# Weighting and turning the prompt's attention outputs during the sample's scores, in a four-layer decoder step on one core

## The chip, the cores and the metric

The program runs on one core of a Trainium2 chip. The metric is the device time of one execution in microseconds (us), the median of several runs; lower is better.

## What is computed

One inference step of a four-layer trunk for two groups of tokens that share the weights: a prompt of 512 tokens and a sample of 8 sequences with 4 new tokens each, 544 columns in all. Layers 0 and 3 are attention layers, layer 1 is a gated delta rule, layer 2 a pooling; each is followed by an MLP. Only the attention layers matter here. Cut to that:

```python
for g, (window, dil) in enumerate(((128, 1), (512, 4), (2048, 16))):   # 3 groups of 6 heads of 64
    q, k, v = rope(qkv[g, 0]), rope(qkv[g, 1]), qkv[g, 2]
    o, lse = dilated_window_prompt(q, k, v, window, dil)     # prompt: no cache
    o, lse = dilated_window_sample(q, k, v, cache_g, window, dil)   # sample: cached keys and values
wts = softmax(stack(lses), over the 3 groups)                # per token and head
y = (stack(outs) * wts).reshape(B, T, 1152) @ w_out          # out-projection, 1152 -> 1024
```

## The kernel before

Activations lie transposed, channels on the 128 partitions and the 544 tokens along the row. Every large product is done in three float32r passes: each operand is split into a high part (a Copy on ScalarE, `act_hi` or `w_hi`) and the rest (a subtraction on VectorE, `act_lo` or `w_lo`), and `pe_tile` (L210) multiplies hi by hi, lo by hi and hi by lo. A weight tile has `t.kt` blocks of 128 rows (9 in the out-projection) and is done by two matmuls of 272 columns for each pass and block, six matmuls a block. `sp_weights` loads the raw weights on SyncE's queue, `act_split` (L188) and `dve_split` (L195) split them two tiles ahead.

The engines have queues of their own in an order written out by hand, and meet at semaphores. In an attention layer (`MixA`) that order is, for each engine:

1. In-projection: 27 weight tiles in 9 units (3 groups by 3 pairs of heads), with the prompt's attention of one unit worked in between the tiles of the next. The prompt's outputs lie unweighted in `a_o` (tokens on the partitions), the negative maxima and sums of their softmax in `a_st`. The new keys and values leave in `prompt_rows` and `sample_rows` on SyncE's queue.
2. The sample's scores: 12 units of cached keys (`K_UNITS`: units 0 and 1 of group 0, units 2 to 9 of group 1, units 10 and 11 of group 2). TensorE does `turn_keys(i + 1)` (L926: 12 transposes of 128x128 from the cache buffer `s_kv` to `misc[1]` to `misc[3]`), then `sample_scores(i)` (L939 and L944). ScalarE copies the three turned tiles of each unit to `s_kT` (L1085), and `turn_keys(i + 2)` waits until the three copies of unit i + 1 are done. VectorE masks the scores and takes the maxima once for each of six pairs of group and batch (L1218 to L1223), ScalarE takes the exponentials (L1071). GpSimd issues the loads of the next cached keys and values into five buffers.
3. The sample's weights: `combine(0, 2, ...)` (L1231 to L1244, one exponential of ScalarE in its middle at L1091) and the scaling of the sample's probabilities (L1252).
4. On TensorE the sample's probabilities are turned (L962, L966) and multiplied with the cached values (L974, L978, L985). Meanwhile VectorE combines the prompt's weights. Group 0 holds tokens in natural order on the partitions, groups 1 and 2 in order modulo 4, so the softmax numbers go through DRAM (`scratch0`, `scratch1`) and come back in the other order (`a_stx0`, `a_stx1`); SyncE issues that between the mask's load and the first out-projection weights. Then VectorE weights `a_o` in place (L1263).
5. The sample's outputs are turned (L993), and split to `act_hi` (L1109) and `act_lo` (L1268).
6. The prompt's outputs: nine tiles f, each turned by four transposes (L1001) to `misc[f % 2]`, split by ScalarE (L1112) and VectorE (L1272) straight from there. Tile f waits until VectorE is through with tile f - 2. `prompt_cols` writes tiles 0 to 2 as they lie and tiles 3 to 8 with a step of four elements (16 bytes).
7. TensorE waits for all nine `act_lo` tiles, then does the eight weight tiles of the out-projection (`a_out`), each evacuated by VectorE's addition to `x` (L1278). The norm and the MLP follow.

## Time and profile before

| | |
|---|---|
| median of 3 runs | 3223.58 us (3214.03 to 3229.64) |
| the profiled execution's own time | 3220.44 us |
| its span, first to last instruction | 3218.6 us |
| busy: TensorE, VectorE, ScalarE, GpSimd | 94%, 44%, 29%, 19% |
| mean granted TensorE clock | 0.926 of full |

The time outside the span is 1.84 us. In the rows "PE" is TensorE's matmul, "PEld" its weight load, DVE is VectorE, ACT ScalarE, POOL GpSimd, SPq SyncE's DMA queue. L followed by a number is a line of the kernel. A row of instructions in order of time reads: start us, us, engine, line, operation, out<-in, xcount, and in brackets the idle time before it and what ended it. PEclk is the share of the full clock that was granted, 0.50 and 1.00 being its two levels, 1.2 and 2.4 GHz. Attention stage 2 runs from 270.68 to 321.79 us in layer 0 and from 2643.43 to 2694.31 us in layer 3.

### The profile page before, as it was taken

What the parts mean: (1) busy time and instruction counts of PE and PEld (TensorE: products, weight loads), DVE (VectorE), ACT (ScalarE), POOL (GpSimd) and SP (SyncE); (2) the same over time, 40 slices, a digit from 0 to 9 for tenths busy, and PEclk for the clock granted to TensorE, in tenths of its full rate; (3) what the DMA queues carried; (4) which work ended last, traced back from release to release, by engine and by line L of the source; (5) the groups of instructions that cost most, each with busy time, mean ns of one, the idle gap of its engine ahead of it and who ended that gap; (6) DMA issues with size and microseconds to landing.
All of it is one profiled execution on the core that took longest, in us unless ns stands there. A gap on an engine that the chain in (4) does not pass through costs nothing.

```text
span 3218.6 us, 55286 instructions
## 1 busy us (share of the span) xinstructions
PE 3019.4 (94%) x24181; PEld 2832.1 (88%) x24181; DVE 1403.1 (44%) x1904; ACT 933.9 (29%) x1634; POOL 616.6 (19%) x518
## 2 busy tenths in 40 slices
PE   7998799999999899999999993999999988899998
PEld 6996599999999777768999993999999983899998
DVE  4552443334675322243433347443356542443332
ACT  5554222222334211112322221222225542322222
POOL 0001141123210111002321142322140002322213
PEclk9998799999999866668999995999999988999999
DMA  3236333343323000212333330443332246234332
GB/s 106 74 89 187 109 99 125 124 131 115 95 75 82 2 1 1 54 53 60 119 120 124 122 113 24 130 128 125 120 124 64 83 133 193 61 120 127 123 125 98
DMA packets 440935, 318.48 MB, mean 99 GB/s; under 512 B 17181, under 2 KB 427470, under 8 KB 438359
## 3 DMA queue, kind: packets, MB, share of 16 engines
q1 hardware_dynamic: 430967, 277.19, 28.4%
q0 software_dynamic: 9728, 37.75, 3.7%
q8 instruction: 191, 3.13, 0.4%
q14 instruction: 49, 0.40, 0.0%
HBM read 299.62 MB, written 71.68 MB: 115 GB/s over the span
## 4 chain that ended last, share of the span: by engine, by line
PE 86%; DVE 6%; ACT 3%; issue 2%; DMA 2%; SPq 1%; POOL 0%; ACTq 0%; DVEq 0%; POOLq 0%
PE acc L210 66%; PE acc L939 2%; PE misc L926 1%; PE misc L1677 1%; PE misc L1678 1%; PE misc L883 1%; PE acc L1665 1%; PE misc L1628 1%; PE acc L1664 1%; PE misc L1639 1%; PE misc L1526 1%; PE acc L1680 1%; DMA s_kv<-cache_a_kv 1%; ACT a_sw L1063 1%; PE misc L829 1%
## 5 line engine op out<-in xcount | busy, mean ns | idle before, releaser
L210 PE MATMUL acc<-act_hi,w_hi 128*128 128x272 f32 x3856 | 814.7, 293 | 22.0 <-DVE act_lo L260 14.2
L210 PE MATMUL acc<-act_lo,w_hi 128*128 128x272 f32 x3856 | 800.4, 289 | 0.0
L210 PE MATMUL acc<-act_hi,w_lo 128*128 128x272 f32 x3856 | 800.1, 289 | 0.0
L195 DVE TENSOR_TENSOR w_lo<-w_raw,w_hi 128x1024 fp32r<-128x1024 f32 (+1 forms) x367 | 583.2, 1589 | 314.1 <-ACT w_hi L188 312.6
L210 PEld LDWEIGHTS acc<-act_hi,w_hi 128*128 128x128 f32 x3856 | 605.9, 189 | 29.3 <-issue 14.5
L210 PEld LDWEIGHTS acc<-act_lo,w_hi 128*128 128x128 f32 x3856 | 607.5, 189 | 0.0
L210 PEld LDWEIGHTS acc<-act_hi,w_lo 128*128 128x128 f32 x3856 | 607.0, 189 | 0.0
L188 ACT ACTIVATE w_hi<-w_raw 128x1024 fp32r<-128x1024 f32 (+1 forms) x367 | 388.0, 1057 | 737.5 <-PE acc L210 675.5
L210 PE MATMUL acc<-h_hi,w_hi 128*128 128x272 f32 x2048 | 425.5, 289 | 0.0
L210 PE MATMUL acc<-h_lo,w_hi 128*128 128x272 f32 x2048 | 422.4, 287 | 0.0
L210 PE MATMUL acc<-h_hi,w_lo 128*128 128x272 f32 x2048 | 421.9, 287 | 0.0
L441 POOL TENSOR_TENSOR h<-relu_t 128x544 f32<-128x544 f32 x128 | 140.2, 1096 | 1044.6 <-DVE relu_t L425 1044.6
L210 PEld LDWEIGHTS acc<-h_lo,w_hi 128*128 128x128 f32 x2048 | 323.0, 188 | 0.0
L210 PEld LDWEIGHTS acc<-h_hi,w_hi 128*128 128x128 f32 x2048 | 319.6, 188 | 0.1
L210 PEld LDWEIGHTS acc<-h_hi,w_lo 128*128 128x128 f32 x2048 | 319.7, 188 | 0.0
L429 DVE TENSOR_TENSOR x<-acc,x 128x544 f32<-128x544 f32 x128 | 92.8, 725 | 396.1 <-PE acc L210 396.1
L404 ACT ACTIVATE h_hi<-relu_t 128x544 fp32r<-128x544 f32 x128 | 84.5, 661 | 556.5 <-DVE relu_t L425 556.5
L425 DVE SCALAR_TENSOR_TENSOR relu_t<-acc,R 128x544 f32<-128x544 f32 x128 | 92.7, 724 | 226.3 <-PE acc L210 214.6
L444 POOL TENSOR_TENSOR h_lo<-h,h_hi 128x544 fp32r<-128x544 f32 x128 | 174.4, 1363 | 10.0
L276 POOL TENSOR_TENSOR sumsq<-sumsq,sq 128x544 f32<-128x544 f32 x56 | 106.0, 1893 | 4.4
L274 POOL TENSOR_TENSOR sq<-x 128x544 f32<-128x544 f32 x56 | 63.6, 1135 | 203.6 <-DVE x L429 97.9
L1063 ACT ACTIVATE a_sw<-acc 32x544 f32<-32x544 f32 x144 | 88.8, 616 | 45.1 <-PE acc L210 43.1
(361 smaller groups left out, 2738.2 us busy)
## 6 DMA issues: line engine op xcount, KB each, us to landing
w_raw<-mlp_w SPq DMA_DIRECT2D x256, 512.0 KB, 3.9
new_a_kv_s<-cache_a_kv SPq DMA_DIRECT2D x128, 381.0 KB, 4.5
s_kv<-cache_a_kv POOLq DMA_DIRECT2D x40, 768.0 KB, 6.1
w_raw<-a_w_in SPq DMA_DIRECT2D x54, 512.0 KB, 4.1
w_raw<-b_w_in SPq DMA_DIRECT2D x32, 512.0 KB, 4.1
w_raw<-a_w_out SPq DMA_DIRECT2D x16, 576.0 KB, 4.0
s_kv<-cache_a_kv POOLq DMA_DIRECT2D x32, 192.0 KB, 4.0
new_a_kv_s<-cache_a_kv SPq DMA_DIRECT2D x16, 372.0 KB, 4.6
```

The source lines that it names most:

```text
L188: nc.scalar.activation(w_hi[:, t.slot, 0:t.kt, :], w_raw[:, t.raw, 0:t.kt, :], ACT.Copy).then_inc(w_hi_done, 1)
L195: nc.vector.tensor_tensor(w_lo[:, t.slot, 0:t.kt, :], w_raw[:, t.raw, 0:t.kt, :], w_hi[:, t.slot, 0:t.kt, :].bitcast(F32), ALU.subtract).t ...
L210: last = nc.tensor.matmul(acc[:, t.first % 2, s, 0:HALF], w[:, t.slot, k, :], a[:, k, s * HALF:(s + 1) * HALF], start=(k == 0 and i == 0), ...
L274: nc.gpsimd.tensor_tensor(sq[:, :], x[:, k, :], x[:, k, :], ALU.mult).then_inc(sq_done, 1)
L276: last = nc.gpsimd.tensor_tensor(sumsq[:, :], sumsq[:, :], sq[:, :], ALU.add)
L404: nc.scalar.activation(h_hi[:, p % 16, :], relu_t[:, p % 2, :], ACT.Square).then_inc(h_hi_done, 1)
L425: nc.vector.scalar_tensor_tensor(halves(relu_t[:, p % 2, :]), acc_of(t), 0.0, halves(R[:, :]), ALU.max, ALU.mult).then_inc(evac_done, 1)
L429: nc.vector.tensor_tensor(halves(x[:, k, :]), acc_of(t), halves(x[:, k, :]), ALU.add).then_inc(evac_done, 1)
L441: nc.gpsimd.tensor_tensor(h32[:, p % 2, :], relu_t[:, p % 2, :], relu_t[:, p % 2, :], ALU.mult).then_inc(h32_done, 1)
L444: nc.gpsimd.tensor_tensor(h_lo[:, p % 16, :], h32[:, p % 2, :], h_hi[:, p % 16, :].bitcast(F32), ALU.subtract).then_inc(h_ready, 1)
L939: nc.tensor.matmul(acc[rows, batch, 0, 0:S_LEN[g]], a_qbd[:, 3 * g + p, b, :], s_kT[:, i % 2, p, keys], start=(p == 0), stop=(p == PAIRS - 1))
L1063: last = nc.scalar.activation(halves(a_sw[32 * (q ^ 1):32 * (q ^ 1) + 32, :]), acc[32 * q:32 * q + 32, t.first % 2, :, 0:HALF], ACT.Copy)
```

## The change

The softmax numbers are sent through DRAM at the end of stage 1 instead of after it. The prompt's weights are combined and `a_o` is weighted within stage 2, on VectorE after the masks 0 and 1; ScalarE does the two exponentials of it after the copies of key units 2 and 3. TensorE turns the nine prompt tiles within stage 2 too, from unit 5 on, one before and one after a unit's scores (the ninth alone), through the one PSUM bank `misc[0]`; VectorE copies each back in place (`turn_back`). The wait for the last `a_vtok` and `a_ktok` rows to leave goes from ScalarE and SyncE to VectorE's mask 0. The sample's weights are combined after mask 5 as before, now as the third of the three. Stage 6 loses its transposes; ScalarE and VectorE split from `a_o` in SBUF. TensorE's first out-projection tile waits for `act_lo` block by block (`k_ready`) instead of for all nine.

```diff
@@ SyncE
+                    if u == NU:
+                        sp.wait_ge(a_probs, 18 * (n + 1))
+                        sp.dma_start(scratch0[a]..., a_st[:, 0, :, :]).then_inc(a_bounce, 16)
+                        for g in (1, 2):
+                            sp.dma_start(scratch1[a]..., a_st[:, g, :, :]).then_inc(a_bounce, 16)
                     if u >= 1:
                         prompt_rows(u - 1)
...
                 sp.wait_ge(a_ocopy, 18 * (n + 1))
-                sp.wait_ge(a_vout, 16 * NU * (n + 1))
-                sp.wait_ge(a_kout, 16 * NU * (n + 1))
                 sp.dma_start(s_mask[:, :, :], aps["c_smask"]).then_inc(a_landed, 16)
-
-                sp.wait_ge(a_probs, 18 * (n + 1))
-                sp.dma_start(scratch0[a]..., a_st[:, 0, :, :]).then_inc(a_bounce, 16)
...
+                sp.wait_ge(a_bounce, 80 * n + 48)
+                sp.dma_start(a_stx0[:, :, :], scratch0[a]...).then_inc(a_bounce, 16)
+                sp.dma_start(a_stx1[:, :, :], scratch1[a]...).then_inc(a_bounce, 16)
@@ TensorE
+                def turn_o(f):
+                    pe.wait_ge(a_scaled, 3 * n + f // 3 + 1)
+                    if f >= 1:
+                        pe.wait_ge(a_turned, 9 * n + f)
+                    for b in range(QT):
+                        last = nc.tensor.transpose(misc[0][:, b * P:(b + 1) * P], a_o[:, f // 3, b, (f % 3) * P:(f % 3 + 1) * P], ident[:, :])
+                    last.then_inc(a_oT, 1)
+
                 turn_keys(0)
                 for i in range(12):
+                    f = 2 * (i - 5)
                     if i < 11:
                         turn_keys(i + 1)
+                    if 0 <= f < FT:
+                        turn_o(f)
                     sample_scores(i)
+                    if 0 <= f < FT - 1:
+                        turn_o(f + 1)
+                pe.wait_ge(a_turned, 9 * (n + 1))
...
-                for f in range(FT):
-                    pe.wait_ge(a_scaled, 3 * n + f // 3 + 1)
-                    if f >= 2:
-                        pe.wait_ge(a_olo, 9 * n + f - 1)
-                    for b in range(QT):
-                        last = nc.tensor.transpose(misc[f % 2][:, b * P:(b + 1) * P], a_o[...], ident[:, :])
-                    last.then_inc(a_oT, 1)
-                pe.wait_ge(a_olo, 9 * (n + 1))
                 pe.wait_ge(s_lo, 12 * (n + 1))
                 for o in range(KD):
-                    pe_tile(pe, WeightTile("a_out", l, o), act_hi, act_lo, k_used=...)
+                    pe_tile(pe, WeightTile("a_out", l, o), act_hi, act_lo, k_ready=(a_olo, 9 * n) if o == 0 else None, k_used=...)
@@ ScalarE
-                act.wait_ge(a_vout, 16 * NU * (n + 1))
-                act.wait_ge(a_kout, 16 * NU * (n + 1))
                 for i in range(13):
...
+                    if i in (2, 3):
+                        combine_exp(i - 2, QT * HG)
+
+                combine_exp(2, 2)
...
+                act.wait_ge(a_turned, 9 * (n + 1))
                 for f in range(FT):
-                    act.wait_ge(a_oT, 9 * n + f + 1)
-                    nc.scalar.activation(prompt_cols(act_hi, f), misc[f % 2]..., ACT.Copy).then_inc(a_ohi, 1)
+                    nc.scalar.activation(prompt_cols(act_hi, f), turned(f), ACT.Copy).then_inc(a_ohi, 1)
@@ VectorE
+                def turn_back(f):
+                    dve.wait_ge(a_oT, 9 * n + f + 1)
+                    nc.vector.tensor_copy(turned(f), misc[0]...).then_inc(a_turned, 1)
+
+                sample_mask(0)
+                sample_mask(1)
+                dve.wait_ge(a_bounce, 80 * (n + 1))
...
+                combine(0, QT * HG, [st[0][0]] + x1[0], [st[1][0]] + x1[1], grid)
+                combine(1, QT * HG, [x0[0]] + st[0][1:], [x0[1]] + st[1][1:], grid)
...                                              # a_o weighted in place, three instructions
+                turn_back(0)
+                sample_mask(2)
+                for f in range(1, FT):
+                    turn_back(f)
+                for k in range(3, 6):
+                    sample_mask(k)
+                dve.wait_ge(s_probs, 6 * (n + 1))
+                combine(2, 2, ...)               # and the scaling of s_p, as before
...
                 for f in range(FT):
                     dve.wait_ge(a_ohi, 9 * n + f + 1)
-                    nc.vector.tensor_tensor(prompt_cols(act_lo, f), misc[f % 2]...,
+                    nc.vector.tensor_tensor(prompt_cols(act_lo, f), turned(f),
                                             prompt_cols(act_hi, f).bitcast(F32), ALU.subtract).then_inc(a_olo, 1)
@@ new
+        def turned(f):
+            return a_o[:, f // 3, :, (f % 3) * P:(f % 3 + 1) * P]
```

## Rows read from the trace of the kernel before

**Rows 1.** The page's chain of work that ended last, shares by engine.
```profile
PE 86%; DVE 6%; ACT 3%; issue 2%; DMA 2%; SPq 1%; POOL 0%; ACTq 0%; DVEq 0%; POOLq 0%
```

**Rows 2.** Stretches of layer 0: length, busy of PE, PEld, DVE, ACT, POOL; PEclk, DMA share, GB/s.
```profile
270.68:321.79 51.11, 47.81 (x432) 29.36 (x432) 5.91 (x20) 21.96 (x46) 11.16 (x17) 0.93 0.70 202
...
363.60:377.68 14.08, 6.80 (x38) 4.65 (x36) 9.24 (x14) 9.74 (x13) 0.00 (x0) 0.74 0.01 2
```

**Rows 3.** The chain in order of time, the last split before the out-projection.
```profile
376.55 1.09 DVE act_lo L1272
```

**Rows 4.** The sample's last splits and first evacuations, in both layers.
```profile
363.36 0.91 ACT L1109 ACTIVATE act_hi<-misc 64x48 fp32r<-64x48 f32 x4 [0.47 <-PE misc L993]
...
386.05 0.73 DVE L1278 TENSOR_TENSOR x<-acc,x 128x544 f32<-128x544 f32 x1 [7.17 <-PE acc L210]
...
2738.39 0.91 ACT L1109 ACTIVATE act_hi<-misc 64x48 fp32r<-64x48 f32 x4 [0.47 <-PE misc L993]
...
2761.63 0.72 DVE L1278 TENSOR_TENSOR x<-acc,x 128x544 f32<-128x544 f32 x1 [7.24 <-PE acc L210]
...
2768.38 0.72 DVE L1278 TENSOR_TENSOR x<-acc,x 128x544 f32<-128x544 f32 x1 [3.64 <-PE acc L210]
```

**Rows 5.** TensorE in the score stage of layer 0, one unit of group 1.
```profile
294.76 1.53 PE L926 MATMUL misc<-ident,s_kv 128*128 128x128 f32 x12
296.22 2.76 PE L939 MATMUL acc<-s_kT,a_qbd 128*32 128x512 f32 x6
...
299.10 1.53 PE L926 MATMUL misc<-ident,s_kv 128*128 128x128 f32 x12
```

**Rows 6.** VectorE: mask 2; a copy of a full PSUM bank; the weighting (ns min/median/max).
```profile
299.28 0.69 DVE L1218 TENSOR_TENSOR s_p<-acc,s_mask 128x512 f32<-128x512 f32 x1 [17.16 <-PE acc L944]
...
300.86 0.15 DVE L1223 TENSOR_SCALAR a_sst<-a_t 128x1 f32<-128x1 f32 x1
...
L1158 DVE COPY a_vtok<-misc x18: 682/684/685, 66.4 to 2633.7; 128x512 f32<-128x512 f32 x18
...
L1263 DVE TENSOR_TENSOR a_o<-a_o,a_f x6: 1750/1752/1759, 338.4 to 2714.2; 128x1536 f32<-128x1536 f32 x6
```

**Rows 7.** The prompt's splits (ns min/median/max), ScalarE copies back to back, one from SBUF.
```profile
L1112 ACT ACTIVATE act_hi<-misc x18: 591/1078/1100, 364.3 to 2751.0; 128x512 fp32r<-128x512 f32 x18
...
L1272 DVE TENSOR_TENSOR act_lo<-misc,act_hi x18: 681/1062/1079, 364.9 to 2752.1; 128x512 fp32r<-128x512 f32 x18
...
282.57 1.55 ACT L1085 ACTIVATE s_kT<-misc 128x512 f32<-128x512 f32 x3
...
376.31 1.17 ACT L188 ACTIVATE w_hi<-w_raw 128x1152 fp32r<-128x1152 f32 x1
```

**Rows 8.** The MLP's first tile, fed block by block, and its stretch.
```profile
434.89 0.49 PE L210 MATMUL acc<-act_hi,w_hi 128*128 128x272 f32 x2 [1.60 <-DVE act_lo L260]
...
435.46 0.41 PE L210 MATMUL acc<-act_hi,w_lo 128*128 128x272 f32 x2
...
434.00:437.00 3.00, 1.66 (x11) 1.47 (x12) 3.00 (x4) 2.84 (x3) 2.79 (x2) 1.00 0.00 0
```

**Rows 9.** The way through DRAM: issue of the return; DMA issues, KB, us to landing.
```profile
279.82 0.34 SPq L782 DMA_DIRECT2D a_stx<-scratch  x1
...
new_a_kv_p<-a_vtok SPq DMA_DIRECT2D x1, 256.0 KB, 8.7
...
a_stx<-scratch SPq DMA_DIRECT2D x1, 48.0 KB, 5.3
```

**Rows 10.** VectorE in layer 0: mask 0 starts, mask 1 ends.
```profile
278.68 0.29 DVE L1218 TENSOR_TENSOR s_p<-acc,s_mask 128x128 f32<-128x128 f32 x1 [8.11 <-PE acc L944]
...
281.96 0.15 DVE L1223 TENSOR_SCALAR a_sst<-a_t 128x1 f32<-128x1 f32 x1
```

**Rows 11.** Stretches of layer 0, columns as in rows 2: the clock around two thin places.
```profile
370.00:371.00 1.00, 0.13 (x1) 0.16 (x2) 0.72 (x1) 0.99 (x1) 0.00 (x0) 0.68 0.00 0
...
319.00:321.00 2.00, 0.23 (x8) 0.23 (x12) 0.86 (x4) 2.00 (x7) 0.75 (x1) 1.00 0.94 353
```

More of the change, by code:

```diff
@@ L994, in pe @@
                     last.then_inc(s_oT, 1)
-                for f in range(FT):
-                    pe.wait_ge(a_scaled, 3 * n + f // 3 + 1)
-                    if f >= 2:
-                        pe.wait_ge(a_olo, 9 * n + f - 1)
-                    for b in range(QT):
-                        last = nc.tensor.transpose(misc[f % 2][:, b * P:(b + 1) * P], a_o[:, f // 3, b, (f % 3) * P:(f % 3 + 1) * P], ident[:, :])
-                    last.then_inc(a_oT, 1)
-                pe.wait_ge(a_olo, 9 * (n + 1))
                 pe.wait_ge(s_lo, 12 * (n + 1))
                 for o in range(KD):
-                    pe_tile(pe, WeightTile("a_out", l, o), act_hi, act_lo, k_used=in_used if o == KD - 1 else None)
+                    pe_tile(pe, WeightTile("a_out", l, o), act_hi, act_lo, k_ready=(a_olo, 9 * n) if o == 0 else None, k_used=in_used if o == KD - 1 else None)
             @staticmethod
@@ L1209, in dve, with sample_mask @@
                             nc.vector.tensor_tensor(halves(a_v[:, u % 2, :]), acc_of(t), halves(R[:, :]), ALU.mult).then_inc(evac_done, 1)
-                for k in range(6):
+                def sample_mask(k):
                     g, batch = k // 2, k % 2
@@ L1216, in dve @@
                         dve.wait_ge(a_landed, 64 * (n + 1))
+                        dve.wait_ge(a_vout, 16 * NU * (n + 1))
+                        dve.wait_ge(a_kout, 16 * NU * (n + 1))
                     o, L = S_OFF[g], S_LEN[g]
@@ L1245, in combine @@
                     chain(dve, last)
-                dve.wait_ge(s_probs, 6 * (n + 1))
-                combine(0, 2, [a_sst[:, 0, g, :] for g in range(NG)], [a_sst[:, 1, g, :] for g in range(NG)], lambda ap: ap)
-                for batch in range(2):
-                    for g in range(NG):
-                        part = s_p[:, batch, S_OFF[g]:S_OFF[g] + S_LEN[g] + NS]
-                        last = nc.vector.tensor_scalar(part, part, a_f[:, 0, g, batch:batch + 1], None, ALU.mult)
-                    last.then_inc(s_pscaled, 1)
-                dve.wait_ge(a_back, 32 * (n + 1))
+                def turn_back(f):
+                    dve.wait_ge(a_oT, 9 * n + f + 1)
+                    nc.vector.tensor_copy(turned(f), misc[0][:, :].rearrange("p (b i) -> p b i", i=P)).then_inc(a_turned, 1)
+                sample_mask(0)
+                sample_mask(1)
+                dve.wait_ge(a_bounce, 80 * (n + 1))
                 grid = lambda ap: ap.rearrange("p (b h) -> p b h", h=HG)
@@ L1271, in dve @@
                     dve.wait_ge(a_ohi, 9 * n + f + 1)
-                    nc.vector.tensor_tensor(prompt_cols(act_lo, f), misc[f % 2][:, :].rearrange("p (b i) -> p b i", i=P),
+                    nc.vector.tensor_tensor(prompt_cols(act_lo, f), turned(f),
                                             prompt_cols(act_hi, f).bitcast(F32), ALU.subtract).then_inc(a_olo, 1)
```

35 lines of the change are left out of this document (17 added, 18 removed).

## The prediction, made before the changed kernel was run

> **What bounds the kernel now.** I read the chain of work that ended last first: TensorE holds 86% of it [rows 1], so the time is TensorE's, and a change helps only where it shortens a stretch in which TensorE waits, or the work on it. The stretches show such a place: in layer 0 from 363.60 to 377.68 us TensorE is busy 6.80 of 14.08 us, at a mean clock of 0.74, while VectorE (9.24) and ScalarE (9.74) take turns [rows 2]. This is stage 6: transposes, high part and low part hand over to one another through two PSUM banks, and the chain in order of time goes through all three; its last link before the out-projection is an `act_lo` [rows 3]. The score stage is the opposite: TensorE is busy 47.81 of 51.11 us, VectorE only 5.91, ScalarE 21.96 [rows 2]. So the change takes work from a stretch where nobody is full and puts it where TensorE is full and the others have room. What it puts on TensorE there is paid in full.
>
> **The gain in stages 6 and 7.** I measure from the end of the sample's high parts to the first evacuation of the out-projection. Before: 363.36 + 0.91 = 364.27 to 386.05 is 21.78 us in layer 0, 2739.30 to 2761.63 is 22.33 us in layer 3 [rows 4].
>
> After, ScalarE starts on tile 0 at once, since the turned tiles have long been there. Tiles 0 to 2 took 0.59 us each, tiles 3 to 8 1.08 [rows 7]. Back to back such copies start about 0.48 us apart where one takes 0.60 (three in 1.55), so they overlap by about 0.1. The source is now SBUF. The nearest row is the weight split, which reads SBUF: 1.17 us for 1152 elements [rows 7]. Against 0.59 for 512 from PSUM that is 0.58 us for 640 elements more, 0.9 ns each, so the other source shows no price beside the elements. I take 3 x 0.5 + 6 x 1.04 = 7.8 us to the last high part; the slow writes come from the step of four elements, which stays. VectorE follows one tile behind, 1.06 us for the last [rows 7]: 8.9. It needs at most 3 x 0.68 + 6 x 1.06 = 8.4 us on its own, so it does not become the bound. The last block's six matmuls take 435.46 + 0.41 - 434.89 = 0.98 us when they come alone [rows 8], and the semaphores on both sides some 0.2. The first evacuation comes 10.1 us after the start. TensorE's nine blocks take 6.75 us at full clock, evacuation to evacuation (2761.63 to 2768.38 [rows 4]), 0.75 a block; they start at 1.4 and so are behind the splits. Gain: 21.78 - 10.1 = 11.7 and 22.33 - 10.1 = 12.2, together 23.9 us.
>
> Bounds. If a subtraction between two SBUF operands costs 0.68 also for tiles 3 to 8, and ScalarE's copy likewise 0.59, TensorE is the bound: 1.4 + 6.75 + 0.2 = 8.4 us, 1.7 more gain for each layer. If both lose from reading SBUF as they lose from the step, 0.4 us a tile, it is 3.6 less for each. I take the middle, since rows 7 show the cost on the strided tiles and not on the others. Weight tiles 0 and 1 are split by then; tile 2's split comes behind the last `act_hi` and `act_lo` and has a tile of 6.75 us in front of it.
>
> **What TensorE pays in the score stage.** A unit of group 1 lasts 299.10 - 294.76 = 4.34 us without a gap on TensorE [rows 5]; twelve transposes take 296.22 - 294.76 = 1.46. Four take 0.49, nine times four 4.4 us a layer. Then waits. Tile f waits for VectorE's copy of tile f - 1: 0.18 to start (299.10 to 299.28 [rows 5, 6]), 0.68 for the copy [rows 6], as much back as there, 1.0 us. Between two tiles lie a unit's scores (2.88) or a `turn_keys` (1.46), so this is hidden, except once: VectorE does mask 2 ahead of `turn_back(1)`. Mask 2 is done 300.86 + 0.15 - 299.10 = 1.91 us after unit 5's scores [rows 5, 6], the copy 2.8 after; TensorE is back after 0.49 + 1.46 = 1.95 and waits 0.84 us with `turn_o(2)`. Sum: 5.2 us a layer, 10.4 in both. Bounds: 4.4 if that wait vanishes behind other slack; 7.9 if each of the nine hand-overs also shows 0.3 us.
>
> **What is put at nothing, and what hides it.** ScalarE's two exponentials (about 0.25 us each) stand in front of the copies of units 3 and 4. This is the place where something is queued behind a wait. Mask 1 ends at 282.11, the first half of the combine is five small instructions, by the 0.15 of the smallest kind and their gaps an estimated 1 us [rows 10], so the exponential is through by 283.4, where ScalarE began its copies of unit 3 at 282.57 [rows 7]. They then end near 284.9, and TensorE wants them at 294.76 - 2 x 4.34 = 286.08. Slack about 1.2 us, nothing paid. The second exponential comes by 286.0, ahead of copies which began after that. VectorE's weighting is 3 x 1.75 = 5.3 us [rows 6], done near 293, its first third near 290; the first tile is wanted at 296.2. All copies back (nine times 0.68) lie in VectorE's empty time.
>
> The way through DRAM: before, the return was issued at 279.82 [rows 9]. Now the three writes go out when the last probabilities are done, near 262, and the return follows the mask's load near 272. With 5.3 us to landing, or even 8.7, the longest near row [rows 9], it is there at 278 to 281, before 282.11. The last prompt rows are issued some 1.0 us later than before and, at 8.7 us to landing, are out by about 274; VectorE's mask 0, which now waits for them, starts at 278.68 [rows 10]. The four DMAs of `a_w_out` that stood behind the return go out some 7 us earlier, and GpSimd's loads of keys have a whole round of five buffers of slack. In stages 3 to 5 nothing on TensorE's way changes: the sample's combine still follows mask 5, and the prompt's combine and weighting there lay beside the value products.
>
> **Sum.** -23.9 + 10.4 = -13.5 us, on the profiled execution 3220.44 - 13.5 = 3206.9. That execution is 3.1 us below the median of the runs shown, so I forecast 3223.6 - 13.5 = 3210 us.
>
> **The clock, a rule against this change.** In stage 6 TensorE was thinly busy and kept the full clock until about 370.5, then fell to 1.2 GHz [rows 11], and was still there when the out-projection began. In the new first tile it is busy 0.75 of each 1.04 us, denser than the MLP's first tile, busy 1.66 of 3.00 at a clock of 1.00 [rows 8]. By these rows it keeps 2.4 GHz. The Trainium skill ("TensorE: Matmul & The Clock Gate", section "HAM oscillation — how this bites in real kernels" and the one after it) says that a stream of matmuls broken by waits between its groups can be throttled again and again. That rule would take the tile to the lower clock; rows 8 speak against it here, and it is a rival below.
>
> **Rivals.**
> - *More gain (22%).* The splits from SBUF run at 0.6 to 0.7 us throughout: 3.4 us more, and without the 0.84 us wait 1.7 more: -17 to -18.6, 3205 to 3207 us. For it: most of the change's work meets free engines. Against it: the step of four elements stays.
> - *The first tile runs at 1.2 GHz (12%).* Nine blocks at 1.5 us are 13.6, from 1.4 on: 15.2 instead of 10.1, so 5.1 lost for each layer, -3.3 in all, 3220 us. For it: after the sample's last transposes TensorE pauses about 2 us, and the clock fell in such company at 370.5. Against: a full queue at the lower clock is just what raised it before.
> - *Hand-overs cost more, or ScalarE is held up by the return from DRAM (11%).* Nine exposed hand-overs are 2.7 us a layer; a return that lands after 283.3 pushes the copies of unit 3, and TensorE, microsecond by microsecond. -5 to -8, 3216 to 3219 us. The longest landing seen nearby would have to grow by over 2 us.
> - *Slower (5%).* The waits of `turn_o` pull the clock down within the score stage. From unit 6 on four units of group 1 and two of group 2 at half clock would add some 4 x 4.3 + 4 = 21 us a layer, 42 in all: 3223.6 - 13.5 + 42 = 3252. It decides as soon as the lower clock lasts for more than a third of those units (6.7 us lost in each layer eats the gain). Against it: a stretch in which TensorE was busy 0.23 of 2.00 us kept a clock of 1.00 [rows 11], and the new wait is 0.84.
>
> **From these to the numbers.** The likeliest case, -10 to -16 us, has 50%. A change under 0.5%, 16 us, can't be told from none in this kernel. The forecast lies just inside. Faster by more: the 22% and a quarter of the likeliest case's edge, 0.34. Slower: 0.05 and a little for the runs' spread, 0.06. Same: 0.60. The range goes from the full extra gain with the spread of a median, 3203, to the first tile at the lower clock, 3219.
>
> **What would show it.** Right: no transposes between the sample's last turn and the out-projection; 10 us from the last sample `act_hi` to the first evacuation in both layers; a score stage of 56.3 us instead of 51.1; one wait of TensorE near 0.8 us on a copy to `a_o`; a clock of 1.00 through the first out-projection tile. Wrong: TensorE waiting for `s_kT` at unit 4, waits before more than one `turn_o`, PEclk of 0.50 after unit 6, or strided splits at 0.7 or at 1.4 us.

## The result, and the profile after

The kernel before took 3225.46 us (median of 15 runs, 3207.31 to 3229.64), the changed kernel 3212.69 us (15 runs, 3191.60 to 3218.03). The ratio is 0.9956, 95% interval [0.9940, 0.9972]: faster by 14 us, 9 to 19 by the interval. In a second job beside other kernels it was 0.9964 [0.9947, 0.9981]. The forecast was 3210 us, 13.5 us less than before, with 0.60 on a change of less than 0.5%.

The page of the changed kernel, its span and its busy time by engine, and the share of the chain that ended last, answering to [rows 1]:

```profile
span 3210.9 us, 55305 instructions
PE 3014.7 (94%) x24181; PEld 2830.3 (88%) x24181; DVE 1414.4 (44%) x1922; ACT 932.0 (29%) x1634; POOL 615.7 (19%) x518
PE 85%; DVE 6%; ACT 3%; issue 2%; DMA 2%; SPq 1%; POOL 0%; ACTq 0%; DVEq 0%; POOLq 0%
```

Nothing on the page tells of the change. It shows in two stretches of layer 0, with the columns of [rows 2]: the score stage, and the stretch from the sample's last high part to the first evacuation.

```profile
272.75:329.40 56.65, 51.93 (x444) 33.33 (x448) 21.51 (x60) 22.45 (x48) 11.13 (x17) 0.92 0.64 186
373.20:383.40 10.20, 8.69 (x58) 7.58 (x59) 9.51 (x12) 8.56 (x11) 0.00 (x0) 1.00 0.00 1
```

VectorE now works 21.5 us in the score stage where it had 5.9. (The first row stops short of the last score matmuls: the stage ends at 329.83, 57.08 us after its start, for 51.1 before and 56.3 foreseen.) In the last stretch TensorE is busy 8.69 of 10.20 us, and the first out-projection tile lies in it; the 6.80 of 14.08 us before were transposes only, and the whole tile followed. To set times beside each other I cut each attention layer at four instants of the trace: the start of the first transpose of the cached keys, the start of the last score matmuls (L944, here L943), the end of the sample's last high part, and the start of the first evacuation of the out-projection.

| us, layer 0 / layer 3 | scores | values, sample's split | to first evacuation | together |
|---|---|---|---|---|
| before | 50.77 / 50.53 | 42.82 / 45.34 | 21.78 / 22.33 | 115.37 / 118.20 |
| after | 56.71 / 55.72 | 43.73 / 43.98 | 10.17 / 10.23 | 110.61 / 109.93 |
| after, second job | 56.80 / 55.70 | 43.04 / 44.19 | 10.25 / 10.19 | 110.09 / 110.08 |
| foreseen change | +5.2 / +5.2 | 0 | -11.7 / -12.2 | -6.5 / -7.0 |

The two layers give 4.76 + 8.27 = 13.0 us back. The profiled executions, 3220.44 and 3212.69 us, differ by 7.7 only, because the rest of the program took 5.3 us more in this pair. That is less than the spread of one kernel's own executions, and it is why the sum is checked by stretches, and the total by medians.

The last stretch on TensorE, ScalarE and VectorE (start us, us, engine, line, operation, count, and in brackets the idle time and what ended it):

```profile
373.21 7.43 ACT L1115 ACTIVATE act_hi<-a_o 128x512 fp32r<-128x512 f32 x9
373.87 1.89 DVE L1289 TENSOR_TENSOR act_lo<-a_o,act_hi 128x512 fp32r<-128x512 f32 x3 [0.44 <-ACT act_hi L1115]
374.71 0.49 PE L210 MATMUL acc<-act_hi,w_hi 128*128 128x272 f32 x2 [1.99 <-DVE act_lo L1289]
...
375.96 6.09 DVE L1289 TENSOR_TENSOR act_lo<-a_o,act_hi 128x512 fp32r<-128x512 f32 x6 [0.20 <-ACT act_hi L1115]
...
378.12 0.30 PEld L210 LDWEIGHTS acc<-act_hi,w_hi 128*128 128x128 f32 x2 [0.19 <-DVE act_lo L1289]
...
383.36 0.72 DVE L1295 TENSOR_TENSOR x<-acc,x 128x544 f32<-128x544 f32 x1
```

The nine high parts follow each other without a gap in 7.43 us. The low parts of tiles 3 to 8 take 6.09 us, 1.02 each, and TensorE stands 0.19 us before a block (PEld is its weight load): the splits set the pace. From tile 3 on it is VectorE that does, for its six low parts follow each other without a wait and end at 382.05, 1.4 us after ScalarE's last high part.

The score stage, one unit of group 1 with its two tiles of `a_o`, answering to [rows 5]:

```profile
303.26 1.47 PE L925 MATMUL misc<-ident,s_kv 128*128 128x128 f32 x12
305.48 0.63 PE L952 MATMUL misc<-ident,a_o 128*128 128x128 f32 x4 [0.74 <-DVE a_o L1254]
...
309.41 1.47 PE L925 MATMUL misc<-ident,s_kv 128*128 128x128 f32 x12
310.72 0.60 PE L952 MATMUL misc<-ident,a_o 128*128 128x128 f32 x4
...
314.62 1.47 PE L925 MATMUL misc<-ident,s_kv 128*128 128x128 f32 x12
```

From `turn_keys` to `turn_keys` it is 314.62 - 309.41 = 5.21 us, where it was 4.34: eight transposes cost 0.87, four 0.435. The wait with `turn_o(2)` is there, 0.74 us, and it is the only one before a `turn_o`. It costs more than its length: the unit that holds it takes 309.41 - 303.26 = 6.15 us, 0.94 more than the next. Without a wait the turn starts 0.16 us before `turn_keys` ends (310.72 for 309.41 + 1.47); that overlap is lost as well.

One thing in the score stage was not foreseen. SyncE's queue in layer 0 (for a DMA issue the second number is how long the issue held the queue):

```profile
264.61 1.21 SPq L772 DMA_DIRECT2D scratch<-a_st  x2
265.86 3.04 SPq L762 DMA_DIRECT2D new_a_kv_p<-a_ktok  x1
268.95 1.81 SPq L762 DMA_DIRECT2D new_a_kv_p<-a_vtok  x1
270.80 1.36 SPq L750 DMA_DIRECT2D new_a_kv_s<-a_kns  x1
...
277.31 0.37 SPq L779 DMA_DIRECT2D s_mask<-c_smask  x1
```

The three writes of prompt and sample rows behind the scratch writes held the queue for 3.04, 1.81 and 1.36 us; in the kernel before they take 0.53, 0.79 and 0.53. Of the kernel before, the first of these writes, the mask's load, and TensorE's wait at `turn_keys(3)`:

```profile
262.75 0.53 SPq L761 DMA_DIRECT2D new_a_kv_p<-a_ktok  x1
...
272.13 0.37 SPq L775 DMA_DIRECT2D s_mask<-c_smask  x1
...
281.77 1.50 PE L926 MATMUL misc<-ident,s_kv 128*128 128x128 f32 x12 [0.74 <-ACT s_kT L1085]
```

The mask's load goes out 4.6 us after the first `turn_keys` (277.31 - 272.75), where it was 1.5 (272.13 - 270.68). What then waits, on VectorE, ScalarE and TensorE of layer 0 and TensorE of layer 3:

```profile
281.92 0.29 DVE L1223 TENSOR_TENSOR s_p<-acc,s_mask 128x128 f32<-128x128 f32 x1 [9.26 <-DMA s_mask<-c_smask]
282.88 0.43 ACT L1076 ACTIVATE s_p<-s_p,a_sst 128x160 f32<-128x160 f32 x1 [3.13 <-DVE a_sst L1228]
283.31 1.55 ACT L1092 ACTIVATE s_kT<-misc 128x512 f32<-128x512 f32 x3
285.00 1.50 PE L925 MATMUL misc<-ident,s_kv 128*128 128x128 f32 x12 [1.48 <-ACT s_kT L1092]
2654.47 1.50 PE L925 MATMUL misc<-ident,s_kv 128*128 128x128 f32 x12 [2.76 <-ACT s_kT L1092]
```

Mask 0 waits for its load, the sample's first exponential for mask 0, the copies of unit 2 stand behind that exponential in ScalarE's queue, and `turn_keys(3)` waits for the copies: 1.48 and 2.76 us, 0.74 in either layer before. It starts 12.25 us after the first `turn_keys` in layer 0 and 11.27 in layer 3, for 11.09 and 10.85 before. The profile names ScalarE as the releaser; the cause is a DMA three steps back, and the chain that ended last says so:

```profile
277.31 4.53 DMA s_mask<-c_smask
283.40 1.46 ACT s_kT L1092 x3
285.00 1.50 PE misc L925 x12
```

### The profile page after: what moved, and what is told of

Its sections match the earlier page's. It is cut to its first block, busy times and chain, and to the rows that moved or that the text cites. A ratio compares the mean times of both kernels' runs of the same rounds, so it can differ in the third digit from the quotient of the medians.

```text
span 3210.9 us, 55305 instructions
## 1 busy us (share of the span) xinstructions
PE 3014.7 (94%) x24181; PEld 2830.3 (88%) x24181; DVE 1414.4 (44%) x1922; ACT 932.0 (29%) x1634; POOL 615.7 (19%) x518
## 4 chain that ended last, share of the span: by engine, by line
PE 85%; DVE 6%; ACT 3%; issue 2%; DMA 2%; SPq 1%; POOL 0%; ACTq 0%; DVEq 0%; POOLq 0%
PE acc L210 66%; PE acc L938 1%; PE misc L1697 1%; PE misc L1698 1%; PE misc L1648 1%; PE acc L1685 1%; PE acc L1684 1%; PE misc L1659 1%; PE misc L1546 1%; PE acc L1700 1%; PE misc L882 1%; DMA s_kv<-cache_a_kv 1%; ACT a_sw L1068 1%; PE misc L828 1%; ACT a_p L1024 1%
## 5 line engine op out<-in xcount | busy, mean ns | idle before, releaser
L210 PEld LDWEIGHTS acc<-act_hi,w_hi 128*128 128x128 f32 x3856 | 606.1, 189 | 29.3 <-issue 18.9
L444 POOL TENSOR_TENSOR h_lo<-h,h_hi 128x544 fp32r<-128x544 f32 x128 | 174.2, 1361 | 10.1
```

The source lines that it names most:

```text
L210: last = nc.tensor.matmul(acc[:, t.first % 2, s, 0:HALF], w[:, t.slot, k, :], a[:, k, s * HALF:(s + 1) * HALF], start=(k == 0 and i == 0), ...
L444: nc.gpsimd.tensor_tensor(h_lo[:, p % 16, :], h32[:, p % 2, :], h_hi[:, p % 16, :].bitcast(F32), ALU.subtract).then_inc(h_ready, 1)
```

## The experiments

My theory: the gain is that TensorE gets tile 0 block by block from tiles turned before; the cost is the transposes put on a full TensorE, and two waits, one for `turn_back(1)` behind mask 2, one for the late mask. Rivals: one of the two parts of the change makes the gain alone; the hand-overs (each tile's wait for the copy of the one before) cost more than the transposes; the splits from SBUF, not the hand-overs, are what could still be cut. All ratios are to the kernel before in runs of the same job. The stretches, for all kernels:

| us, layer 0 / layer 3 | scores | values, sample's split | to first evacuation | ratio, 95% interval |
|---|---|---|---|---|
| kready_only | 49.08 / 48.89 | 43.36 / 43.89 | 19.04 / 18.89 | 0.9980 [0.9965, 0.9994] |
| move_only | 57.01 / 55.81 | 43.58 / 43.88 | 18.08 / 17.81 | 1.0022 [1.0009, 1.0036] |
| turn_twice | 60.39 / 60.40 | 48.52 / 43.12 | 10.23 / 10.21 | 0.9993 [0.9972, 1.0014] |
| rows_after_mask | 55.46 / 55.46 | 43.69 / 44.37 | 10.18 / 10.18 | 0.9956 [0.9941, 0.9970] |
| permute | 57.54 / 58.30 | 43.18 / 43.08 | 10.08 / 10.10 | 0.9967 [0.9954, 0.9980] |
| mask_order | 54.80 / 54.58 | 43.25 / 45.71 | 10.23 / 10.24 | 3210.73 us, one run |
| gaps_rows | 50.75 / 49.04 | 42.90 / 46.27 | 10.24 / 10.18 | 0.9933 [0.9911, 0.9956] |
| best | 50.94 / 48.88 | 43.39 / 46.81 | 10.09 / 8.55 | 0.9934 [0.9912, 0.9955] |
| gaps_only | 51.98 / 51.17 | 43.63 / 45.98 | 11.30 / 10.24 | 0.9938 [0.9914, 0.9961] |
| gaps_rows_again | 50.72 / 50.61 | 42.88 / 47.17 | 10.30 / 10.23 | 0.9942 [0.9921, 0.9962] |

The score stage has a spread of its own: in some executions the second `turn_keys` takes 2.79 us at half clock, in others 1.51 at full clock, and the code there is the same. Where no late mask stands behind it, the faster start shortens the stage by about 1.6 us (layer 3 of gaps_rows, 49.04, beside 50.61 in gaps_rows_again); both layers of kready_only have it.

**Each part alone.** To the kernel before, only the tile-by-tile start:

```diff
-                pe.wait_ge(a_olo, 9 * (n + 1))
                 pe.wait_ge(s_lo, 12 * (n + 1))
                 for o in range(KD):
-                    pe_tile(pe, WeightTile("a_out", l, o), act_hi, act_lo, k_used=in_used if o == KD - 1 else None)
+                    pe_tile(pe, WeightTile("a_out", l, o), act_hi, act_lo, k_ready=(a_olo, 9 * n) if o == 0 else None, k_used=in_used if o == KD - 1 else None)
```

> The kernel before with one part of the change: the first out-projection tile waits for act_lo block by block; the transposes stay in stage 6. Theory: the nine transposes still go one after another through two banks, so tile 0 can start only behind the last of them, about 2 us earlier than before: the first evacuation about 19.5 us after the last sample act_hi instead of 21.8, -2 us a layer, -4 in all, ratio 0.9988. Rival: the block-by-block wait is what made the change faster, and brings 5 us or more a layer by itself: ratio 0.997 or less.

And the whole change but for that: the wait for `a_olo` stays and `k_ready` is left out.

> The changed kernel with the wait for all nine act_lo tiles put back; the prompt tiles are still turned in the score stage. Theory: splits done 8.8 us after the last sample act_hi, then a whole first tile, partly at 1.2 GHz: first evacuation at 16 to 17 us instead of 10.2, so +6 to +7 us a layer over the changed kernel, which with the longer score stage leaves nothing of the gain: ratio to before 0.9995 to 1.001. Rival: the move out of stage 6 carries the gain and the finer wait adds a microsecond or two: ratio 0.996 to 0.997.

The tile-by-tile start alone took 3216.55 us beside 3224.17. It cuts the last stretch by 2.7 and 3.4 us, to 19.0 and 18.9 where 19.5 was expected; the rival of 5 us or more a layer is out. The transposes still alternate with the splits through the two banks, at half clock by then (first line), and two hand-overs further the next four start:

```profile
373.81 1.09 PE L1001 MATMUL misc<-ident,a_o 128*128 128x128 f32 x4 [0.40 <-DVE act_lo L1271]
374.93 1.10 ACT L1111 ACTIVATE act_hi<-misc 128x512 fp32r<-128x512 f32 x1 [0.40 <-PE misc L1001]
375.76 1.09 PE L1001 MATMUL misc<-ident,a_o 128*128 128x128 f32 x4 [0.87 <-DVE act_lo L1271]
```

The move alone was slower than before, 3228.09 us, and a little slower than its expected range. Its splits are as fast as those of the changed kernel, but TensorE stands idle through all nine and then starts at the lower clock (second and third line: two stretches of layer 0, the seventh number is TensorE's clock):

```profile
379.88 0.82 PE L210 MATMUL acc<-act_hi,w_hi 128*128 128x272 f32 x2 [9.24 <-DVE act_lo L1290]
...
380.00:386.00 6.00, 6.00 (x31) 6.00 (x32) 1.09 (x1) 0.00 (x0) 0.00 (x0) 0.60 0.33 98
386.00:390.00 4.00, 4.00 (x35) 4.00 (x33) 0.72 (x1) 0.75 (x1) 0.00 (x1) 1.00 0.00 0
```

The last stretch shrinks by 3.7 and 4.5 us, and the score stage takes 5 to 6 more. I had looked for 16 to 17 us in the last stretch and found 18; the rest is the clock, whose mean of 0.60 over these 6 us is 2.4 us lost, more than I had allowed for. So the parts are worth -3 and -4 us in the last stretch each by itself, -12 together: the move makes the splits continuous, and only the tile-by-tile start lets TensorE use them and keeps it at work.

**The price of a transpose.** Eight transposes for each tile in place of four, the second four into the same place:

```diff
-                    for b in range(QT):
+                    for b in (0, 1, 2, 3, 0, 1, 2, 3):
```

> The changed kernel with the four transposes of each prompt tile issued twice in the score stage (same result). Theory: TensorE is full there and pays each transpose: 36 more at 0.122 us are 4.4 us a layer, 8.8 in all over the changed kernel, ratio to before about 0.998. Rival: they lie partly in issue gaps or waits, and less than 4 us in all is added: ratio 0.9965 or less.

The unit with two tiles grew from 5.21 to 6.08 us, 0.435 for each four again: linear, 0.109 us each. The wait before `turn_o(2)` fell from 0.74 to 0.31, as four more transposes lie ahead of it:

```profile
304.73 1.06 PE L952 MATMUL misc<-ident,a_o 128*128 128x128 f32 x8 [0.31 <-DVE a_o L1254]
...
309.54 1.47 PE L925 MATMUL misc<-ident,s_kv 128*128 128x128 f32 x12
...
315.62 0.60 PE L925 MATMUL misc<-ident,s_kv 128*128 128x128 f32 x4
```

No other hand-over shows a wait, here or in the changed kernel, and that takes the rival of exposed hand-overs out. The score stage took 3.7 and 4.7 us more, nine times 0.435 being 3.9: TensorE pays here in full. The ratio is 0.0037 higher, 12 us, which the two intervals leave uncertain by some 8 us. In layer 0 of the profiled execution the middle stretch was 4.8 us longer: the waits for cached values grew from 3.2 to 5.6 us, and TensorE was busy 2.4 us more at a lower mean clock (0.68 for 0.72). Whether the doubled transposes are the cause isn't shown; in layer 3 the stretch did not grow.

**The late mask.** The last prompt rows first, then the scratch writes, the mask, the return, and the last sample rows after that:

```diff
-                    if u == NU:
-                        sp.wait_ge(a_probs, 18 * (n + 1))
-                        sp.dma_start(scratch0[a].rearrange("(b p) c -> p b c", p=P), a_st[:, 0, :, :]).then_inc(a_bounce, 16)
...
                     if u >= 1:
                         prompt_rows(u - 1)
-                        if u % PAIRS == 0:
+                        if u % PAIRS == 0 and u < NU:
                             sample_rows(u // PAIRS - 1)
+                sp.wait_ge(a_probs, 18 * (n + 1))
+                sp.dma_start(scratch0[a].rearrange("(b p) c -> p b c", p=P), a_st[:, 0, :, :]).then_inc(a_bounce, 16)
...
                 sp.dma_start(a_stx1[:, :, :], scratch1[a].rearrange("(b p) c -> p b c", p=P)).then_inc(a_bounce, 16)
+                sample_rows(NG - 1)
```

> The changed kernel with another order on SyncE's queue: the last prompt rows first, then the three writes through DRAM, the mask's load and the return, and the last 16 sample rows behind them. Theory: in the changed kernel the prompt rows' issue behind the small-packet writes took 3.04 and 1.81 us and put the mask's load 3 us later, so mask 0 and the copies of unit 2 were late and TensorE waited 1.48 and 2.76 us instead of 0.74 at turn_keys(3); with this order it waits 0.8 or less there, -0.7 and -2.0 us: ratio to before about 0.9948, 0.0008 under the changed kernel. Rival: the late mask costs nothing since its wait lies where another one is: no difference from the changed kernel and the same wait.

SyncE's queue and the wait of TensorE in layer 0:

```profile
263.84 0.64 SPq L773 DMA_DIRECT2D scratch<-a_st  x1
264.52 4.70 SPq L775 DMA_DIRECT2D scratch<-a_st  x2
270.43 0.35 SPq L778 DMA_DIRECT2D s_mask<-c_smask  x1
...
281.51 1.50 PE L925 MATMUL misc<-ident,s_kv 128*128 128x128 f32 x12 [0.74 <-ACT s_kT L1092]
```

The mask goes out before the first `turn_keys` (at 270.50 here), and the wait is back at 0.74 (0.7 in layer 3). That shows the cause of the wait. The slow issue has moved, not gone: now two of the scratch writes themselves, behind the prompt rows, hold the queue 4.70 us. In the kernel before, behind the mask's load and 2.4 us after the last sample row, they took 1.22. Common to both slow orders is that the scratch writes (pieces of 12 numbers) and the prompt rows (256 KB each) stand next to each other in the queue; why that holds it is open. The time is 3209.55 us and the ratio, 0.9956, is that of the changed kernel: 1.2 us in the sum of the stretches doesn't show in it, and 0.9948 had been expected. In layer 3 the stage is only 0.3 us shorter, since the changed kernel had the faster start there and this one had not.

**The wait with mask 2.** To this version, `turn_back(1)` ahead of mask 2:

```diff
                 turn_back(0)
+                turn_back(1)
                 sample_mask(2)
-                for f in range(1, FT):
+                for f in range(2, FT):
```

> The changed kernel with turn_back(1) ahead of mask 2 on VectorE. Theory: TensorE's wait of 0.74 us before turn_o(2) goes (the copy is then back 1.0 us after its transposes, inside turn_keys), and mask 2, 0.7 us later, delays ScalarE's exponential and its copies of unit 7, which end some 3 us before they are wanted. Rival: the wait comes back as one for s_kT at the next turn_keys.

```profile
301.84 0.60 PE L952 MATMUL misc<-ident,a_o 128*128 128x128 f32 x4
302.37 2.76 PE L938 MATMUL acc<-s_kT,a_qbd 128*32 128x512 f32 x6
```

`turn_o(2)` follows without idle time, and the score stage is 0.7 and 0.9 us shorter: mask 2 in VectorE's queue was the cause, and the wait was paid in full, near the 0.94 us read above.

**The step of four elements.** The order of the columns is changed already when the turned tile is copied back, so that both splits write contiguously:

```diff
-                    nc.vector.tensor_copy(turned(f), misc[0][:, :].rearrange("p (b i) -> p b i", i=P)).then_inc(a_turned, 1)
+                    nc.vector.tensor_copy(back_out(f), back_in(f, misc[0])).then_inc(a_turned, 1)
...
+        def back_out(f):
+            return turned(f) if f < PAIRS else turned(f).rearrange("p c (j r) -> p r c j", r=QT)
+        def back_in(f, bank):
+            if f < PAIRS:
+                return bank[:, :].rearrange("p (b i) -> p b i", i=P)
+            return bank[:, :].rearrange("p (r c j) -> p r c j", r=QT, c=QT)
...
         def prompt_cols(buf, f):
-            if f < PAIRS:
-                return buf[:, f, 0:SEQ].rearrange("p (b i) -> p b i", i=P)
-            return buf[:, f, 0:SEQ].rearrange("p (i b) -> p b i", b=QT)
+            return buf[:, f, 0:SEQ].rearrange("p (b i) -> p b i", i=P)
```

> The changed kernel, with tiles 3 to 8 put in token order by VectorE's copy back in the score stage (a step of four elements there), so that ScalarE and VectorE split all nine tiles without a step. Theory: the step alone made the splits of tiles 3 to 8 cost 1.0 us instead of 0.6, and they set the pace of the first out-projection tile; now TensorE does, and the first evacuation comes 8.4 to 9 us after the last sample act_hi instead of 10.2 (at the lower clock for 3 us it is the 9.9 side): -1 to -1.8 us a layer, ratio to before 0.9947 against 0.9956. The copies back grow from 0.69 to about 1.07 and stay hidden. Rival: the slower copies push TensorE in the score stage by 0.4 us at each of eight hand-overs and eat it: no gain over the changed kernel.

Splits, first evacuation, and two stretches of tile 0 in layer 0:

```profile
371.83 4.80 ACT L1115 ACTIVATE act_hi<-a_o 128x512 fp32r<-128x512 f32 x9
372.49 5.51 DVE L1289 TENSOR_TENSOR act_lo<-a_o,act_hi 128x512 fp32r<-128x512 f32 x9 [0.44 <-ACT act_hi L1115]
...
381.88 0.72 DVE L1295 TENSOR_TENSOR x<-acc,x 128x544 f32<-128x544 f32 x1 [2.62 <-PE acc L210]
...
375.00:376.00 1.00, 1.00 (x6) 1.00 (x6) 1.00 (x2) 1.00 (x3) 0.00 (x0) 0.50 0.00 0
...
379.00:380.00 1.00, 1.00 (x10) 1.00 (x9) 0.27 (x1) 0.00 (x0) 0.00 (x0) 1.00 0.00 0
```

The splits fell to 0.53 and 0.61 us a tile, from 0.83 and 0.89 on average: the step of four elements is what they cost, and SBUF as source costs ScalarE nothing that shows (0.53 a tile, where three copies from PSUM take 1.55). Yet the first evacuation still comes at 10.1. VectorE is through at 378.0, and after a weight tile's split it waits 2.62 us for TensorE, which is now the bound and ran for over 3 us of the tile at half clock. The same edit in `best` (below) shows the other case: in layer 3 the clock stayed at 1.00 and the evacuation came at 8.55, where 8.4 was worked out for a tile bound by TensorE. In layer 0 it came at 10.09. The ratio, 0.9967, is no better than the changed kernel's; 0.9947 had been expected. The step also isn't hidden where it went: VectorE's copies back of tiles 3 to 8 take 1.07 to 1.10 us for 0.69, and a unit with two such tiles takes 5.38 us (308.08 to 313.46) for 5.21, 0.5 us a layer over three units. The rival had said 0.4 us at each of eight hand-overs.

**Turning where TensorE waits.** After the last scores TensorE waits 5.0 us in each layer for the sample's weights. Tiles 0 to 3 are turned there, each into a bank of its own, and brought back by ScalarE, which is free; tiles 4 to 8 are turned between the value products. SyncE's order is that of rows_after_mask.

```diff
-                    f = 2 * (i - 5)
                     if i < 11:
                         turn_keys(i + 1)
-                    if 0 <= f < FT:
-                        turn_o(f)
                     sample_scores(i)
-                    if 0 <= f < FT - 1:
-                        turn_o(f + 1)
-                pe.wait_ge(a_turned, 9 * (n + 1))
+                for f in range(4):
+                    turn_o(f)
+                pe.wait_ge(a_turned, 9 * n + 4)
...
                 for i, (g, batch, bs) in enumerate(V_UNITS):
+                    for f in {6: (4, 5, 6), 10: (7,), 11: (8,)}.get(i, ()):
+                        turn_o(f)
...
```

> The kernel rows_after_mask with the nine prompt tiles turned elsewhere: four in TensorE's 5.0 us wait behind the last scores (four PSUM banks, ScalarE copies back), three before the 2.4 us wait for the first unit of the second batch's values, one each before the last two value units (VectorE copies back). Theory: TensorE paid 4.6 us a layer for them in the score stage and pays under 1 here, where it waits anyway: score stage back to 51, the stretch from there to the last sample act_hi longer by at most 1 us, -7 to -9 us in all against the changed kernel, ratio to before 0.9930. Rival: the waits aren't free, since each delay of TensorE there delays the release of a cache buffer and with it the next load, or the copies delay the sample's chain: that stretch grows by 4 us or more and the ratio stays at 0.9956.

TensorE's wait in the kernel before, then the four tiles and what is left of the wait in this one:

```profile
326.78 1.54 PE L962 MATMUL misc<-ident,s_p 128*128 128x128 f32 x6 [4.96 <-DVE s_p L1252]
...
321.57 1.97 PE L954 MATMUL misc<-ident,a_o 128*128 128x128 f32 x16
326.64 1.51 PE L974 MATMUL misc<-ident,s_p 128*128 128x128 f32 x6 [3.10 <-ACT a_o L1102]
```

The score stage is back at the length of the kernel before (less than that in layer 3, by the faster start), and the turning takes 1.97 of the 5.0 us; 3.10 are left, 3.5 in layer 3. The ratio is 0.9933, where 0.9930 was expected. With the contiguous splits added:

> Both together: tiles turned in TensorE's waits, and put in token order by the copies back. Theory: gains add, -9 to -12 us against the changed kernel, ratio to before 0.992. Rival: the slower copies back (1.07 us, on ScalarE for tile 3, on VectorE for five) reach TensorE between the value products, where two banks are all there is, and the sum is no better than gaps_rows.

That added nothing that shows (0.9934, for an expected 0.992). To see whether the order of SyncE's queue matters at all, and to set the new version beside the changed kernel on the same chip:

> The changed kernel once more, unedited, beside the version that turns its tiles in TensorE's waits, so that the two share their runs of the kernel before. By its own timing the ratio is 0.9956; I expect 0.995 to 0.997 again.

> Tiles 0 to 3 turned after the last score unit, where TensorE waited 5.0 us for the sample's weights, tiles 4 to 8 between the value products; the order of SyncE's queue is that of the changed kernel, so mask 0 still waits for its late load. Theory (what the change pays is work on a full TensorE, and TensorE's waits can take it): the score stage falls from 56.7 and 55.7 us to about 51.5 and 53, the wait at the turn of unit 3's keys stays at 1.5 and 2.8 us, and the ratio is 0.9940. Rival (the late mask also moves what follows, so that the turned tiles find no gap): the stretch from the last scores to the sample's last high part grows by more than 2 us in layer 0, ratio 0.9955.

> The best version once more beside the changed kernel on the same chip. From the stretches of the traces it should take 6.7 + 4.4 = 11 us less than the changed kernel, ratio to the kernel before 0.992 to 0.994; that is at least 0.002 below the changed kernel of the same job. If the two ratios' intervals overlap by more than half, the gain over the changed kernel can't be told from none.

The changed kernel took 3214.08 us here, ratio 0.9964; without the queue's order 3203.25, 0.9938; with it 3205.06, 0.9942. Two lessons. The order of the queue is worth nothing that shows in the time, though the wait for the late mask is there (1.9 us in layer 0 of gaps_only), and the score stages of gaps_only are 1.3 and 0.6 us longer than those of gaps_rows_again. And turning in the waits is worth 9 and 11 us over the changed kernel by these medians. The intervals of 0.9964 and 0.9942 overlap by 0.0015, less than half of either; of the seven runs of gaps_rows_again all lie below 3207, of the twelve of after_again eleven lie above 3210. I take the gain over the changed kernel as real and its size as uncertain by a few us. By stretches it was 11.2 us in gaps_rows against the changed kernel (some 1.6 of it by the faster start in layer 3), 8.3 in gaps_rows_again and 5.9 in gaps_only against after_again (1.1 lost by the clock in layer 0). What turning costs between the value products shows in layer 3: the middle stretch, from the score matmuls' end to the sample's last high part, in gaps_rows_again and then in after_again (columns of [rows 2]):

```profile
2687.00:2733.80 46.80, 35.93 (x181) 15.55 (x180) 9.96 (x40) 10.59 (x33) 8.89 (x14) 0.78 0.48 150
...
2695.84:2739.65 43.81, 32.23 (x144) 12.13 (x144) 6.59 (x35) 8.63 (x29) 8.87 (x14) 0.73 0.51 159
```

TensorE is busy 3.7 us more, its wait for the sample's weights is 1.5 us shorter, and its waits for cached values did not shrink, 4.1 us for 3.8: the stretch grows by 3.0. In layer 0 those waits fell from 3.0 to 1.9 us, and the stretch is 42.88 us for 43.04: there the turning was free. Why the cached values come no sooner in layer 3 isn't shown.

## Why the prediction was right, step by step

- **The last stretch.** 10.1 us foreseen, 10.17 and 10.23 measured. The terms hold too: 8.9 us to the last low part was 8.86 (373.19 to 382.05). Within that, two small errors cancel: the high parts took 7.43 us for 7.8, and VectorE, which "does not become the bound", did: its nine low parts take 8.0 of the 8.2 us from 373.87 on, and the last comes 1.4 us behind the last high part and not 1.06. By the prediction's own terms, 8.4 us begun one tile late already end at 9.0. The gain was 11.6 and 12.1 us, for 11.7 and 12.2.
- **The score stage.** 5.2 us a layer foreseen, 5.9 and 5.2 measured. The transposes cost 3.9 us for 4.4: I had divided the 1.46 us from one unit's first transpose to its scores by twelve, and that holds the passage to another kind of matmul; twelve with more transposes behind them took 310.72 - 309.41 = 1.31. The wait with `turn_o(2)` was 0.74 us for 0.84, and cost 0.94.
- **What was put at nothing.** This is the step that failed. The slack at the copies of units 3 and 4 was real: the first combine's exponential ran at 285.47 and no copy behind it was late. But the issue of the mask's load was put "near 272" and came at 277.31. Some 2.1 us of that are a layer that began later as a whole (272.75 for 270.68); the other 3.1 are the queue's, because the writes ahead of the mask were counted as some 1 us later and held the queue 4.4 us longer on top, of which a pause that the queue had ahead of the mask before, 1.9 us, took up a part. What it cost is the wait at `turn_keys(3)`, 0.7 us more than before in layer 0 and 2.0 in layer 3. In layer 3 the faster start, 1.6 us less to the third `turn_keys`, made up for most of it; with the mask in time it would have been a gain instead. Put right, the terms in layer 0 are 3.92 for the transposes, 0.94 for `turn_o(2)`, 0.22 up to the third `turn_keys` (it begins 8.06 us after the first and not 7.84, the lower clock having lasted a little longer), 0.94 from there to the fourth (0.74 more wait, and 0.20 because the third took 1.73 and not 1.53 us), and 0.08 less at the last unit's wait: 5.94. In layer 3 they are 3.92 + 0.94 - 1.61 + 2.03 - 0.08 = 5.20. That is what was measured. The foreseen 5.2 was near partly by luck: the transposes were priced too high by 0.5, and the queue, put at nothing, cost 0.7 and 2.0.
- **The clock.** Rows 8 spoke for 2.4 GHz in tile 0, and in layer 0 it was so, 1.00 throughout. In layer 3 it was not (same columns as [rows 2]):

```profile
2746.00:2747.00 1.00, 1.00 (x6) 1.00 (x6) 1.00 (x2) 1.00 (x2) 0.00 (x0) 0.50 0.00 0
...
2749.00:2750.00 1.00, 1.00 (x9) 1.00 (x9) 1.00 (x2) 1.00 (x2) 0.00 (x0) 0.95 0.00 0
```

  From about 2745.7 to 2749.1 TensorE ran at 1.2 GHz and then came back. It had waited 2.0 us for the first block, in layer 0 as well. The first evacuation came at 10.23 all the same: TensorE has 0.3 us to spare in each block at full clock, and the splits set the pace again before the tile ended. That was no exception. Of the 16 such tiles in the profiled executions (two layers each of after, after_again, turn_twice, rows_after_mask, mask_order, gaps_rows, gaps_only and gaps_rows_again) the mean clock over this stretch was 1.00 in 4, 0.83 in 11 and 0.70 in one. The first evacuation came at 10.17 to 10.18 us in the 4 and at 10.19 to 10.30 in the 11. The one at 0.70 is layer 0 of gaps_only: the lower clock lasted from about 366.7 to 373.5, and the evacuation came 1.1 us later, 11.30. So the prediction's argument for the full clock was wrong more often than right, and the rival "the first tile runs at 1.2 GHz" was half right: the clock mostly falls, but does not stay down for the whole tile, and costs 0 to 1.1 us instead of 5.1. It cost so little because the splits set the pace. The lower clock is also what kept the contiguous splits from their gain, 10.1 instead of 8.55. The Trainium skill's rule ("TensorE: Matmul & The Clock Gate", "HAM oscillation — how this bites in real kernels"), that a stream of matmuls with waits between its groups can be throttled repeatedly, agrees with layer 3 and not with layer 0 of the changed kernel, and with 12 of the 16 tiles.
- **More gain (22%).** Its condition, splits of 0.6 us throughout, did not occur; permute made it occur and gained nothing that shows. **Slower (5%)**: nothing of it appeared, the score stage kept a clock of 1.00 from 286.43 to its end. **Hand-overs, or a late return (11%)**: neither came. The combine began at 284.63, right behind mask 1 and without a wait for the return. But ScalarE was held up, by the mask's load instead of the return, which is the rival's mechanism with another cause.
- **Within 0.5% or beyond.** 0.44% is in the likeliest case's range, on the side of "same" where 0.60 stood, with the bound of 0.5% inside the interval. That such a change "can't be told from none in this kernel" was too strong: with 15 runs of each the interval leaves out 1.

Open: why SyncE's queue is held where scratch writes and prompt rows stand together, what decides in which executions the clock falls in tile 0, and why the cached values hold the value products in layer 3 of the kernels that turn in TensorE's waits.

## What to carry to other kernels

Work taken off a stretch of hand-overs pays only if the bound engine can then take the data piece by piece: here each half alone was worth -6 and +7 us of measured time (0.9980 and 1.0022), both together -14. Before moving work ahead, look for a wait of the bound engine, not for a stretch where others have room: nine tiles of transposes cost 3.9 us a layer in the full stretch, and in the wait of 5.0 us behind it four of them cost at most 0.4 us. In a hand-written queue, price a DMA that is moved by how long its issue and the next ones hold the queue in company, and follow every load behind it to the engine that uses it.

## What the runs showed of the hardware

- DMA issues on SyncE's queue are not of fixed length: the same write took 0.53 us before, and 3.04 behind the scratch writes; the pair of scratch writes 1.22 us in the kernel before and 4.70 behind the prompt rows.
- A copy or subtraction of 128x512 that writes with a step of four elements takes about 0.4 us more than one that writes contiguously: 0.97 (7.43 less three of 0.53, by six) against 0.53 on ScalarE, 1.02 against 0.61 on VectorE. VectorE's copy back in the score stage shows it too, 1.07 to 1.10 for 0.69. ScalarE's reading from SBUF instead of PSUM shows no price (0.53 us a tile back to back, for 1.55 / 3 from PSUM).
- Transposes of 128x128 within TensorE's stream cost 0.109 us each at full clock, four more or eight more alike; a wait of 0.74 us in that stream costs 0.94.
- With the same code fed at 1.02 us a block, TensorE's granted clock stayed at 1.00 through the first out-projection tile in 4 of 16 cases and fell to 0.50 for some 3.5 us in 11 and 6.8 us in one.
